# A two-block transformer kernel: block 1's first projections, three pairs of slices as seven block products each

## What is computed

```python
DEPTH, SEQ, D_MODEL, D_FF = 2, 256, 1024, 2816
def _swiglu(x, w1, w3, w2):
    return (jax.nn.silu(x @ w1) * (x @ w3)) @ w2
for l in range(DEPTH):                                   # block 1
    h = _swiglu(x, ffn_w1[l, 0], ffn_w3[l, 0], ffn_w2[l, 0])
    x = _layernorm(ALPHA * x + 0.5 * h, ln_g[l, 0], ln_b[l, 0])
    h = _mixer(x, l, ...)
    x = _layernorm(ALPHA * x + h, ln_g[l, 1], ln_b[l, 1])
    h = _swiglu(x, ffn_w1[l, 1], ffn_w3[l, 1], ffn_w2[l, 1])
    x = _layernorm(ALPHA * x + 0.5 * h, ln_g[l, 2], ln_b[l, 2])
```

## Time and profile before

| | us |
|---|---|
| median of 3 runs (1950.02 to 1951.34) | 1950.27 |
| the profiled execution | 1950.56 |
| span in its profile | 1948.7 |
| TensorE busy in the span | 1919.6 |
| VectorE busy | 1196.0 |
| ScalarE busy | 924.4 |
| mean granted clock of TensorE | 0.999 |

### The profile page before, as it was taken

One profiled execution on the slowest core, in us unless ns is written; L12 is line 12 of the kernel. 1 busy time (PEld: TensorE's weight loads), 2 busy tenths in 40 slices (PEclk: granted clock), 3 DMA queues, 4 the chain that ended last, 5 costly groups with the idle time before them and its releaser, 6 DMA issues.

```text
span 1948.7 us, 24336 instructions
## 1 busy us (share of the span) xinstructions
PE 1919.6 (99%) x9160; PEld 1576.5 (81%) x9160; DVE 1196.0 (61%) x1471; ACT 924.4 (47%) x1147; POOL 101.2 (5%) x168
## 2 busy tenths in 40 slices
PE   9999999999999999999999999989999999999999
PEld 7888888888888788888888888877788887778887
DVE  5555866677445645577667655578755466775545
ACT  5443445545443543443554534357644355654443
POOL 2000100000000100010000000011000000100000
PEclk9999999999999999999999999999999999999999
DMA  9675554546655765565354765465365545346542
GB/s 318 196 226 194 200 191 148 173 152 194 215 189 177 219 227 194 173 224 186 131 172 151 225 206 179 148 173 184 128 234 172 172 170 186 119 147 215 179 165 87
DMA packets 202155, 357.69 MB, mean 184 GB/s; under 512 B 8048, under 2 KB 101152, under 8 KB 201824
## 3 DMA queue, kind: packets, MB, share of 16 engines
q1 hardware_dynamic: 195856, 334.85, 51.5%
q0 software_dynamic: 6224, 21.82, 3.9%
HBM read 353.49 MB, written 1.05 MB: 182 GB/s over the span
## 4 chain that ended last, share of the span: by engine, by line
PE 92%; DVE 5%; DVEq 1%; ACT 1%; issue 0%; DMA 0%; SPq 0%
PE acc L717 52%; PE aux L717 32%; DVE w_low L2160 2%; PE aux L833 2%; PE aux L732 1%; PE aux L987 1%; DVE xT_low L2166 0%; DVE x_res L2248 0%; DMA w_raw<-ffn_w 0%; PE aux L997 0%; PE aux L1033 0%; PE aux L996 0%; PE aux L1011 0%; DVE buf_k L2945 0%; DVE x_res L2241 0%
## 5 line engine op out<-in xcount | busy, mean ns | idle before, releaser
L2160 DVE TENSOR_TENSOR w_low<-w_raw,w_high 128x2048 fp32r<-128x2048 f32 (+1 forms) x304 | 686.6, 2271 | 417.3 <-ACT w_high L1589 415.1
L1589 ACT CAST w_high<-w_raw 128x2048 fp32r<-128x2048 f32 (+1 forms) x312 | 586.7, 1896 | 432.3 <-PE acc L717 324.6
L717 PE MATMUL aux<-w_high,xT_high 128*128 128x512 f32 x960 | 380.6, 396 | 3.7 <-DVE xT_low L2166 1.7
L717 PE MATMUL aux<-w_high,xT_low 128*128 128x512 f32 x960 | 374.6, 390 | 0.0
L717 PE MATMUL aux<-w_low,xT_high 128*128 128x512 f32 x960 | 373.9, 389 | 0.0
L717 PE MATMUL acc<-w_high,yT_high 128*128 128x512 f32 (+1 forms) x836 | 329.5, 394 | 0.4 <-issue 0.4
L717 PE MATMUL acc<-w_high,yT_low 128*128 128x512 f32 (+1 forms) x836 | 325.3, 389 | 0.0
L717 PE MATMUL acc<-w_low,yT_high 128*128 128x512 f32 (+1 forms) x836 | 324.8, 388 | 0.0
L717 PE MATMUL acc<-w_high,xT_high 128*128 128x512 f32 (+2 forms) x752 | 297.6, 396 | 5.2 <-DVE xT_low L2166 4.1
L717 PE MATMUL acc<-w_high,xT_low 128*128 128x512 f32 (+2 forms) x752 | 291.3, 387 | 0.0
L717 PE MATMUL acc<-w_low,xT_high 128*128 128x512 f32 (+2 forms) x752 | 291.1, 387 | 0.0
(11 more groups left out here) (343 smaller groups left out, 1351.5 us busy)
## 6 DMA issues: line engine op xcount, KB each, us to landing
w_raw<-ffn_w SPq DMA_DIRECT2D x174, 512.0 KB
w_raw<-w_ff SPq DMA_DIRECT2D x64, 1024.0 KB
w_raw<-w_in SPq DMA_DIRECT2D x52, 1024.0 KB
w_raw<-ffn_w SPq DMA_DIRECT2D x44, 1024.0 KB
w_raw<-w_branch SPq DMA_DIRECT2D x16, 1024.0 KB
w_raw<-o_w_in SPq DMA_DIRECT2D x12, 1024.0 KB
w_raw<-w_ple_gate SPq DMA_DIRECT2D x8, 1024.0 KB
w_raw<-e_w_in SPq DMA_DIRECT2D x6, 1024.0 KB
```

What stands on the lines that cost most here:

```text
L717: last = nc.tensor.matmul(dst, lhs[:, kt, tok], rhs(j), start=(kt == k_first and q == 0), stop=(kt == k_last and q == 2))
L1589: nc.scalar.copy(whi[:, s, 0:size], raw[:, s, 0:size]).then_inc(slot_hi[s], 1)
L2160: V.tensor_tensor(wlo[:, s, 0:size], raw[:, s, 0:size], cast(whi[:, s, 0:size]), ALU.subtract)\
```

## The change

Of the 11 slices of each feed-forward of block 1, slices 0, 1, 4, 7 and 10 stay as they are (`PLAIN`). Slices 2+3, 5+6 and 8+9 are pairs (`QUADS`). The up product of a pair is a 2x2 block product: two token tiles by two halves of K by two halves of columns (512 of w1, 512 of w3). It was eight block products of 12 matmuls, and is now seven. For that

- four combinations of blocks of x are made once per feed-forward ("forms", `whole`, `combine`, `form_low` on VectorE, casts on ScalarE);
- the four raw weight blocks of a pair are loaded whole into the mixer's buffers `buf_v`, `buf_q`, `buf_u`, `buf_val` (R11, R21, R12, R22) and added up there in place on VectorE (`add_to`), four additions per pair; each of seven units is then split into high and low as before and takes a ring slot;
- the products' sums are finished by `term1` to `term3` in `mix_param` (copies on ScalarE, additions on VectorE), and the pair's hidden values are transposed from there.

The ring has a new order, the last down unit is split like any other, and the norm's and the ring's split instructions at start and end are no longer cut in halves.

```diff
+QUADS = 3
+PLAIN = (0, 1, 4, 7, 10)
+FORMS = 4
...
+            def quad_load(l, which, q, r):
+                freed = {R11: "y", R21: "y", R12: "w", R22: "b22"}[r]
+                if q > 0:
+                    s, n = ffn_unit(l, which, f"{freed}_{q - 1}")
+                    sp.wait_ge(slot_lo[s], n + 2)
...
+                def quad_product(name, q, b, lh, ll, first):
+                    s = lo_wait(f"{name}_{q}")
+                    for k in range(4):
+                        for n, (lhs, rhs) in enumerate(((lh, whi), (lh, wlo), (ll, whi))):
+                            last = nc.tensor.matmul(aux[:, b, :], lhs(k), rhs[:, s, k * NC:(k + 1) * NC],
...
+                hidden(0, 1)
+                for j in range(2):
+                    hidden_unit(1, 0, j)
+                    if j == 1:
+                        plain_T(0)
+                    hidden_unit(1, 1, j)
+                for p in range(2):
+                    pe.wait_ge(acc_read[p], n_acc[p].k + 1)
+                plain_down(0, 0)
+                plain_down(0, 1).then_inc(unit_used, 1)
+                plain_T(1)
+                for q in range(QUADS):
+                    o = 3 * q + 4
+                    quad1(q)
...
+                low_plain("h1_1")
+                low_plain("d0")
+                low_sum("b11", 0, R11)
+                for n in range(FORMS):
+                    form_low(n)
+                if mid is not None:
+                    mid()
+                add_to(0, R11, R12)
+                low_sum("b21", 0, R21)
+                dve.wait_ge(aux_full[2], n_aux[2].k + 1)
+                multiply(1, 0)
+                plain_low_T(0)
+                multiply(1, 1)
...
+                    low_sum("v", q, R11)
+                    plain_low_T(1 if q == 0 else o - 3)
+                    add_to(q, R11, R22)
+                    add_to(q, R12, R22)
+                    low_sum("x", q, R11)
+                    low_plain(f"d{o - 3}")
+                    add_to(q, R11, R21)
+                    low_sum("w", q, R12)
```

More of the change, by code:

```diff
@@ L452, in ffn1 @@
                 else:
-                    hidden1(l, which, 0)
-                down1(l, which, NF - 1, 3, 0)
-                with sp.Fori(0, NF - 1) as i:
-                    hidden1(l, which, i + 1)
-                    down1(l, which, i, 2, i)
+                    hidden1(l, which, 0, 0)
+                    hidden1(l, which, 0, 1)
+                hidden1(l, which, 1, 0)
+                hidden1(l, which, 1, 1)
+                quad_load(l, which, 0, R11)
+                down1(l, which, 0)
+                for r in (R12, R21, R22):
+                    quad_load(l, which, 0, r)
+                for q in range(QUADS):
+                    o = 3 * q + 4
+                    down1(l, which, o - 3)
+                    hidden1(l, which, o, 0)
+                    down1(l, which, o - 2)
+                    down1(l, which, o - 1)
+                    hidden1(l, which, o, 1)
+                    if q + 1 < QUADS:
+                        for r in (R12, R21, R11, R22):
+                            quad_load(l, which, q + 1, r)
+                down1(l, which, NF - 1)
             def mixer_unit(l, u):
@@ L838, in down_part @@
                     s, n = down_slots[q], i
-                    if final and last_slot is not None:
-                        s, n = last_slot, 0
                     if t == 0:
@@ L942, in ffn1 @@
             def ffn1(l, which, next_tile0):
[L943 to L949 removed]
+                aux0 = [c.k for c in n_aux]
@@ new lines, in quad_T @@
+                def quad_T(q):
+                    pe.wait_ge(h_ready, 2 * quads_before(l, which, q) + 2)
+                    pe.wait_ge(aux_read[2], aux0[2] + 2 * q + 2 + 1)
+                    for b in (2, 3):
+                        for f in range(2):
+                            for t, h in enumerate((term2, term3)):
+                                f0 = (2 * (b - 2) + f) * P
+                                last = nc.tensor.transpose(aux[:, b, (2 * f + t) * P:(2 * f + t + 1) * P],
+                                                           h[:, f0:f0 + P], ident[:])
+                        last.then_inc(aux_full[b], 1)
@@ new lines, in down_part @@
+                def down_part(i, t, halves=(0, 1)):
+                    s = FFN_UNIT[f"d{i}"][0]
+                    if t == 0:
+                        lo_wait(f"d{i}")
+                    k0 = 2 if i == NF - 1 else 0 if i in PLAIN else 4 + 2 * ((i - 2) % 3)
+                    vh, vl = (w[:, s, :].rearrange("p (k n) -> p k n", k=2) for w in (whi, wlo))
+                    for half in halves:
+                        col = slice(half * NC, (half + 1) * NC)
+                        last = products(acc[:, half, t, :], [(k0 + k, k) for k in range(2)],
+                                        0 if i == 0 else -1, 3 if i == NF - 1 else -1, yTh, yTl, t,
+                                        lambda k: vh[:, k, col], lambda k: vl[:, k, col])
+                    return last
@@ new lines, in quad_product @@
+                def quad_product(name, q, b, lh, ll, first):
[3 more added lines that the diff above has]
+                            last = nc.tensor.matmul(aux[:, b, :], lhs(k), rhs[:, s, k * NC:(k + 1) * NC],
+                                                    start=(first and k == 0 and n == 0), stop=(k == 3 and n == 2), skip_group_check=not first)
+                    last.then_inc(unit_used, 1)
@@ new lines, in ffn1 @@
+                plain_down(0, 0)
+                plain_down(0, 1).then_inc(unit_used, 1)
+                plain_T(1)
+                for q in range(QUADS):
+                    o = 3 * q + 4
+                    quad1(q)
+                    if q + 1 == QUADS:
+                        break
+                    hidden(o, 0)
+                    quad_T(q)
+                    hidden(o, 1)
+                    for t in range(NT):
+                        last = quad_down(o - 2, t)
+                    last.then_inc(unit_used, 1)
+                    plain_T(o)
+                    for t in range(NT):
+                        last = quad_down(o - 1, t)
+                    last.then_inc(unit_used, 1)
```

649 lines of the change are left out of this document (451 added, 198 removed).

## The result

The changed kernel takes 1984.57 us (median of 4 runs, 1984.39 to 1985.64), the one before 1950.44 beside it: 1.0175 times as long, 95% interval 1.0158 to 1.0193. Forecast were 1975.5 and a range of 1961 to 1987. So the sign and the range held, and the centre is 9.1 us short.

The account below looks back on a forecast made before the run. TensorE, busy 99% of the span, was taken to bound the kernel. -32.6 + 4x(8.0+1.5+1.1+2.0) + 7.4 = +25.2 on the profiled 1950.56 gave 1975.8, or 1975.5 after 0.3 for the median; range 1961 to 1987.

Parts of the forecast that it names:

- Removed matmuls: All pairs of the four feed-forwards: 144 matmuls of 0.2267 us fewer on TensorE, -32.6 us.
- First down product: Start of each feed-forward: TensorE waits for VectorE's first yT_low, +8.0 us, in parts of 1.1, 0.6 and 6.3.
- Pair 0: First pair of each feed-forward: product w waits for VectorE's queue and a ScalarE copy, +1.5 us.
- Later pairs: Pairs after the first: no loss, VectorE at 86%, tightest at product w with a cover of 1.2 us.
- End of tile 0: Slice 10's down product, now directly behind its transposes, waits for their split: +1.1 us per feed-forward.
- First feed-forward: First feed-forward only: position_angles ahead of the addition, +4.2, and slice 0's late down unit, +3.2; +7.4 us more.
- The clock: Behind the gap before the first down product: TensorE falls to half clock, +2.0 us per feed-forward, between 0 and 2.4.
- Uncut low parts at the end: End of feed-forward: cost nothing, hidden by a stretch with VectorE idle half the time; without it up to 1.1.
- 1 (the clock holds): Rival: clock holds or falls only once, the gaps are plain waits; 1967.5 us, chance 0.13.
- 2: Rival: VectorE does the new sums at twice the rate; 1943 us, chance 0.05.
- 3: Rival: additions in place cost more than a low part, 2.7 instead of 2.2 us each; 1986 us, chance 0.06.
- 4: Rival: no wait before the first down product, as TensorE's own order makes it late anyway; 1925 us, chance 0.03.

Follow-up runs that it names:

- the best kernel: e5 with VectorE's idle stretches at the start of a feed-forward filled by work moved earlier; 1937.65 us, 0.9932 of the kernel before.
- e1: Changed kernel with slice 1's multiplies and the first split of hidden values moved directly behind the low part of b11; 1968.0 us.
- b1: Kernel before, plus only four idle differences of 2048 columns on VectorE ahead of slice 0's down unit in each feed-forward of block 1; 1981.63 us.
- e3: Changed kernel with ScalarE's cast of slice 0's down unit moved behind the second Silu and the cast of slice 1's second unit; 1981.13 us.
- e2: Changed kernel with position_angles and its sine moved from the start of the first feed-forward to behind pair 0's split of hidden values; 1981.8 us.
- b2: Kernel before, with only VectorE's order at the end of block 1's feed-forwards made like the changed kernel's; 1960.71 us.
- e4: Changed kernel with the feed-forward's end reordered: next stage's first unit split before tile 0's residual sum, its second in halves, slice 10's transposes earlier; 1974.21 us.
- b3: Kernel before, plus only three idle differences on VectorE ahead of slice 0's down unit, one fewer than b1; 1970.58 us.
- e5: Changed kernel with the four moves of e1, e2, e3 and e4 together; 1944.81 us, 0.9971 of the kernel before.

## Why the prediction was right, and where it was not

- **Removed matmuls, right in count:** 9016. -32.6 us was never seen by itself, since it is paid back in the same stretches; the best kernel's second feed-forward is 3.8 shorter than before, with 3.4 more of waits, 1.68+1.02 of them in pair 0; with 8.2 removed that leaves 1.0 not traced.
- **First down product, right:** gap 6.15 for 6.3, 1.12 and 0.29 for 1.1 and 0.6: 7.6 for 8.0. VectorE's durations and order, read from the kernel before, gave the place and the size of a wait that no trace had shown yet. e1 shows that it is the order there, and b1 that such a wait alone, in the kernel before, costs nearly as much.
- **Pair 0, nearly:** 1.04 for 1.5, before w, in pair 0 alone. Later pairs nothing: right.
- **End of tile 0:** 0.92 for 1.1.
- **First feed-forward, +13.0 for +11.8:** the down unit's cast came at 28.66, not 27.1, and a Silu behind it delayed more. e3 and e2 show both causes, but not at my prices of 3.2 and 4.2: they gained 2.7 and 2.6 in this feed-forward, with waits shorter by 1.1 and 2.8. The forecast of the waits as a whole was 2.3 too high here and that of the clock 2.4 too low.
- **The clock: the mechanism right, the term too small.** This is most of the 9.1 us by which the centre is off: 16.7 for 8.0. I had counted one fall of 2.0 per feed-forward, at most 2.4. In the second it cost 1.5; in the fourth 3.1 behind one gap; the first had two long gaps and lost 4.4, the third lost 1.7 behind the gap of 2.29 at its start and 3.1 behind the one of 6.14. Another 1.4 fell in mixer 0 and 1.5 in block 2. The bound of 2.4 came from a misreading: I had the clock at its lower level for "nearly 5 us" behind the gap of 3.29 in the earlier trace rows; steps of 1 us show it at 0.50 from 1273 to 1276 alone, with 0.90 in the step on either side, so for a little over 3 us. The mean clock is 0.986 for 0.996: I had counted only matmuls that run slowly, and the mean has the idle time at half clock in it, and more falls.
- **Luck in the totals:** the waits of the feed-forwards were forecast 49.8 and measured 43.5, the clock there 8.0 and 13.8. The two errors offset each other, so that feed-forwards 2 and 4 look nearer (4.0 and 4.7 for 4.4) than their terms are.
- **What failed** is the sentence "Uncut low parts at the end, the last down unit on VectorE instead of by DMA, and GpSimd's later loads I cost at nothing", with "what hides them is this same stretch". It hides them for tile 0. I didn't ask what stands behind them on VectorE: tile 1's residual sum and norm, on which the next stage's start hangs, where the kernel before already waited 1.3. They cost 2.7+1.3 in the mixers (1.4 of it is a fall of the clock in the first) and, in the third feed-forward, a wait of 2.29 in place of 1.32 with a fall of the clock. b2 shows it without the rest of the change, e4 by taking it away. The bound I gave, "up to 1.1", was for TensorE waiting on the low part itself, the wrong consumer. Block 2's +1.5 is something else. e4 didn't give it back (the rest of the program takes 679.1 there), and b1, whose end is that of the kernel before, has 1.0 of it. It is the clock behind the gap before block 2, over the 8 us from the next instruction on, before and after:
```profile
1271.20:1279.20 8.00, 7.12 (x35) 0.79 0.46 151
```
```profile
1303.90:1311.90 8.00, 7.33 (x28) 0.59 0.44 150
```
The gap ahead is 3.29 in the one and 3.21 in the other; why the clock stays down for longer, no run shows.
- **Rivals:** 1 (the clock holds) fell with the clock behind the four gaps and with b1, 2 and 3 with additions of 2.28, 4 with the gap.

## What to carry to other kernels

When work is taken from the busiest engine and given to an idler one, sum that engine's queue from the last point where it was free to each thing that the busy one waits for; an average load of 72% says nothing of the first 20 us of a stage. The order of that queue was worth more than the change: the same arithmetic ran 1984.57 and 1937.65. And for each instruction moved toward the end of a stage, ask who stands behind it, not only who waits for it. Price TensorE's new waits together with the clock behind them: here 46.4 us of waits brought 16.7 more of lost clock, behind gaps of 1.6 us as well as of 8.

## What the hardware showed that I had not expected

- In block 1's feed-forwards a gap of 3.0 to 3.2 us before TensorE's next matmul was followed by half clock in three of four, never in the third, in b3 and in e5 alike. Every gap of 5.2 or more was followed by it (8 of 8 in b1 and the changed kernel). Shorter ones were now and then, and not the same in every kernel: at the start of the first mixer 1.64 was in the changed kernel and 1.63 in e1 wasn't, at that of the second 1.54 wasn't and 1.52 in e1 was; the shortest was 1.34, in b2. So the length of the gap alone doesn't tell it. Nor does it tell the price: a fall cost 1.4 to 3.2 us, and behind the same gap of 6.08 in the fourth feed-forward 3.1 in the changed kernel and 1.6 in e2. The Trainium skill, "TensorE: Matmul & The Clock Gate", Part 1, says that for modelling the ramp is under 1% of a span and shouldn't be fitted to a count of slow matmuls. Here a fall is 0.1 to 0.2% of the span, under that bound; but 9.7 us of 30.9 in b1 came on top of its gaps, and in the changed kernel the falls together were half of its loss.
- Instructions of GpSimd and VectorE that each read two SBUF sources don't run beside each other; GpSimd's recorded time holds the waiting too (with 4.6 of its own, 6.3 of the 10.9 and 4.1 of the 8.7), and back-to-back work on VectorE kept it out.
